# A two-layer hybrid decoder step: VectorE's order in two token mixers and the slots of four weight tiles

## What is computed

```python
z = rmsnorm(x) @ w_in                       # columns of four mixers and of their gates
oa = gla(z)        # gated linear attention: a decay for each key channel
ob = retnet(z)     # rotated q and k, a fixed decay for each head
oc = deltanet(z)   # convolution, then the gated delta rule with a triangular inverse
od = ssd(z)        # convolution, then a scalar decay for each head
x = x + (sum_n sigmoid(mg_n) * (o_n @ w_branch_n)) @ w_out
x = x + swiglu(x)  # layer 0 dense, layer 1 the best 2 of 8 experts
x = x + sigmoid(rmsnorm(x) @ ple_w_gate) * (p @ ple_w_proj)
```

## Time and profile before

| | us |
|---|---|
| median of 3 runs (lowest to highest) | 2600.65 (2597.46 to 2604.7) |
| the profiled execution, and its span in the trace | 2596.66, 2594.9 |
| TensorE busy | 2399.1 (92%), mean granted clock 0.944 |
| VectorE busy | 1639.1 (63%) |
| ScalarE busy | 1074.1 (41%) |
| GpSimd busy | 181.1 (7%) |

### The profile page before, as it was taken

One profiled execution on the slowest core, in us unless ns is written; L12 is line 12 of the kernel. 1 busy time (PEld: TensorE's weight loads), 2 busy tenths in 40 slices (PEclk: granted clock), 3 DMA queues, 4 the chain that ended last, 5 costly groups with the idle time before them and its releaser, 6 DMA issues.

```text
span 2594.9 us, 38245 instructions
## 1 busy us (share of the span) xinstructions
PE 2399.1 (92%) x14436; PEld 2069.6 (80%) x14436; DVE 1639.1 (63%) x2112; ACT 1074.1 (41%) x1450; POOL 181.1 (7%) x247
## 2 busy tenths in 40 slices
PE   8899898899999899899798997999999999999996
PEld 6788778876899888789687866787887878878786
DVE  4554853743665454457636633778787887878776
ACT  4332311321333334324122220566666666667662
POOL 0212111201000001202012010000000000000000
PEclk8999898998999989999898988899999999999998
DMA  5323311322444333234112320898898978889871
GB/s 197 105 87 134 131 66 41 111 82 98 152 163 163 127 130 106 95 134 142 54 50 83 110 73 32 325 327 289 300 329 297 335 284 303 319 296 332 291 278 64
DMA packets 122566, 456.43 MB, mean 176 GB/s; under 512 B 14056, under 2 KB 14474, under 8 KB 120018
## 3 DMA queue, kind: packets, MB, share of 16 engines
q1 hardware_dynamic: 118818, 432.66, 47.5%
q0 software_dynamic: 3632, 22.12, 2.4%
HBM read 443.72 MB, written 11.00 MB: 175 GB/s over the span
## 4 chain that ended last, share of the span: by engine, by line
PE 72%; DVE 17%; issue 6%; ACT 4%; POOL 1%; DVEq 0%; DMA 0%; SPq 0%; ACTq 0%; POOLq 0%
PE ps L726 7%; PE ps L728 7%; PE ps L727 7%; PE ps L773 6%; DVE weights_low L2255 4%; PE ps L1293 4%; PE ps L1295 4%; PE ps L1294 4%; PE ps L1315 3%; PE ps L1316 3%; PE ps L1317 3%; PE ps L1266 3%; PE ps L767 2%; DVE arena L1889 2%; PE ps L808 1%
## 5 line engine op out<-in xcount | busy, mean ns | idle before, releaser
L726 PE MATMUL ps<-u_high,tiles_high 128*128 128x288 f32 x1688 | 526.0, 312 | 17.5 <-DVE tiles_low L1718 17.5
L727 PE MATMUL ps<-u_low,tiles_high 128*128 128x288 f32 x1688 | 513.0, 304 | 0.0
L728 PE MATMUL ps<-u_high,tiles_low 128*128 128x288 f32 x1688 | 511.1, 303 | 0.0
L1718 DVE TENSOR_TENSOR tiles_low<-ring,tiles_high 128x1024 fp32r<-128x1024 f32 x238 | 298.1, 1255 | 201.6 <-ACT tiles_high L1374 200.2
L726 PEld LDWEIGHTS ps<-u_high,tiles_high 128*128 128x128 f32 x1688 | 332.1, 197 | 26.7 <-issue 24.6
L2255 DVE TENSOR_TENSOR weights_low<-expert_ring,weights_high 128x1024 fp32r<-128x1024 f32 x288 | 334.5, 1219 | 5.2 <-ACT weights_high L1627 2.0
L727 PEld LDWEIGHTS ps<-u_low,tiles_high 128*128 128x128 f32 x1688 | 332.6, 197 | 0.5
L728 PEld LDWEIGHTS ps<-u_high,tiles_low 128*128 128x128 f32 x1688 | 332.2, 197 | 0.0
L1374 ACT ACTIVATE tiles_high<-ring 128x1024 fp32r<-128x1024 f32 x238 | 250.6, 1054 | 170.9 <-DMA ring<-in_stream 81.0
L1293 PE MATMUL ps<-weights_high,u_high 128*128 128x512 f32 (+1 forms) x768 | 297.6, 388 | 22.9 <-DVE weights_low L2255 22.3
L2255 DVE TENSOR_TENSOR weights_low<-ring,weights_high 128x1024 fp32r<-128x1024 f32 x240 | 280.2, 1218 | 43.2 <-ACT weights_high L1627 42.1
(11 more groups left out here) (381 smaller groups left out, 3290.2 us busy)
## 6 DMA issues: line engine op xcount, KB each, us to landing
ring<-in_stream SPq DMA_DIRECT2D x530, 512.0 KB, 4.2
expert_ring<-in_stream SPq DMA_DIRECT2D x288, 512.0 KB, 5.6
arena<-in_state POOLq DMA_DIRECT2D x8, 1024.0 KB, 5.1
state_s<-arena POOLq DMA_DIRECT2D x8, 1024.0 KB, 4.3
const<-in_const SPq DMA_DIRECT2D x1, 2052.5 KB, 12.0
arena<-in_const POOLq DMA_DIRECT2D x2, 832.0 KB, 4.9
h<-in_x SPq DMA_DIRECT2D x1, 1152.0 KB, 5.0
y<-acc POOLq DMA_DIRECT2D x1, 1152.0 KB, 4.4
```

What stands on the lines that cost most here:

```text
L726: mm(out, hi[k], uh[:, k, :], start=k == 0, stop=False)
L727: mm(out, hi[k], ul[:, k, :], start=False, stop=False)
L728: last = mm(out, lo[k], uh[:, k, :], start=False, stop=k == KD - 1)
L1718: tt(t_low[:, q % HELD, :], ring[:, (t % RING) * TILE:(t % RING + 1) * TILE], t_high[:, q % HELD, :].bitcast(F32), ALU.subtract).then_inc( ...
```

## The change

VectorE in GLA takes the values and clears the banks right behind the first level's differences, ahead of the three lows of slot 0; `qg` and the clearing of `dd` come behind slot 0. VectorE in RET takes only the first of the three branch tiles of slot 0 ahead of the sines and the addition, and the other two behind them. Two slot lists are new. In GDN the tile of slot 29 goes to slot 27 and, dealt out in order, slot 30 gets a tile and slot 38 none. In SSD slots 2 and 5 become empty, slots 7 and 11 get a tile, and slots 13, 17 and 19 have the tile that was in 14, 16 and 18.

```diff
 SLOTS = [
     [3, 1, 2, 1, 1, 1, 1, 0, 1, 0, 1, 1, 1, 1, 1, 1, 1, 2],
     [3, 1, 1, 2, 1, 1, 2, 2, 1, 2],
-    [1, 1, 1, 1, 1, 1, 1, 1, 0, 1, 0, 0, 1, 1, 0, 1, 0, 1, 0, 1, 0, 1, 0, 1, 0, 1, 0, 0, 0, 1, 0,
-     0, 0, 0, 1, 0, 1, 1, 1, 0, 0],
-    [1, 1, 1, 1, 1, 1, 1, 0, 1, 1, 1, 0, 1, 0, 1, 1, 1, 0, 1, 0, 1, 2, 2],
+    [1, 1, 1, 1, 1, 1, 1, 1, 0, 1, 0, 0, 1, 1, 0, 1, 0, 1, 0, 1, 0, 1, 0, 1, 0, 1, 0, 1, 0, 0, 1,
+     0, 0, 0, 1, 0, 1, 1, 0, 0, 0],
+    [1, 1, 0, 1, 1, 0, 1, 1, 1, 1, 1, 1, 1, 1, 0, 1, 0, 1, 0, 1, 1, 2, 2],
 ]
...
-            def fill(L, n, s):
-                for x in FILL[L][n][s]:
+            def fill(L, n, s, lo=0, hi=None):
+                for x in FILL[L][n][s][lo:hi]:
                     lows(T_OF[x] - 1)
                     if x[0] == "br":
                         branch_tile(x)
...
                 for lv, w in enumerate(LEVELS):
-                    if lv == 1:
-                        take_vk(L, GLA)
-                        V.memset(ps_t[:, M:M + 4, 0:PAIR], 0.0).then_inc(cross_zero, 1)
-                        tt(qg[:, 0:2, :], zq[:, :, 256:288], egp[:, 0:2, :], ALU.mult).then_inc(qg_ready, 1)
-                        V.memset(dd, 0.0)
                     if lv >= 2:
                         dve.wait_ge(lev_ps, 6 * L + lv - 1)
...
                     last.then_inc(ldiff_ready, 1)
+                    if lv == 0:
+                        take_vk(L, GLA)
+                        V.memset(ps_t[:, M:M + 4, 0:PAIR], 0.0).then_inc(cross_zero, 1)
                     fill(L, GLA, lv)
+                    if lv == 0:
+                        tt(qg[:, 0:2, :], zq[:, :, 256:288], egp[:, 0:2, :], ALU.mult).then_inc(qg_ready, 1)
+                        V.memset(dd, 0.0)
...
-                fill(L, RET, 0)
+                fill(L, RET, 0, 0, 1)
                 dve.wait_ge(rot_ps, L + 1)
                 tt(z4, ps_t[:, M:M + 4, 0:TOK], C("sin").unsqueeze(1).to_broadcast([P, 4, TOK]), ALU.mult).then_inc(dve_step, 1)
                 dve.wait_ge(dve_step, steps.next())
                 tt(z4, z4, tmp4, ALU.add).then_inc(rope_ready, 1)
+                fill(L, RET, 0, 1)
                 dve.wait_ge(rope_ready, L + 1)
```

## The result

| | before | after |
|---|---|---|
| median of 4 runs each (lowest to highest) | 2600.67 (2597.46 to 2604.7) | 2615.56 (2610.8 to 2619.68) |
| ratio to before, 95% interval | | 1.0067 [1.0052, 1.0082] |
| profiled execution, span | 2596.66, 2594.9 | 2610.8, 2609.0 |
| TensorE busy | 2399.1 | 2417.0 |
| TensorE idle (span less busy) | 195.8 | 192.0 |

What follows compares the result with a forecast made beforehand. TensorE, busy for 92% of the span, was taken as the bound, so only idle time and clock could give anything back. Reorderings -8.7 and slots +8.1 a layer gave -1.2 us in two layers: 2599.5, range 2583 to 2609.

Steps and rivals of the forecast that it cites:

- GLA, -5.5 a layer: GLA's first level: the 4.0 us wait for bank clearing goes, and 1.5 of low clock behind it is regained.
- the low comes late: Rival in GLA: third tile's low late by 1.8, or second level by 1; 5.6 more, 2605.1, chance 0.06.
- the contention I bounded at 1.8: GLA: GpSimd's multiplying might hold VectorE off the values, starting the third tile 1.8 late; 0 was taken.
- I take 1.5 of it as regained: GLA: of 1.7 us lost at clock 0.72 behind the wait, 1.5 comes back without it (0 to 1.7).
- RET, -3.2: RET: TensorE's wait of 3.21 us ahead of the transposes, for the rotation's last step, goes whole in each layer.
- GDN, +0.6: GDN: wait of 1.11 and 2.54 moves one level; output norm's chain shifts +0.6 a layer (-2.0 to +2.6).
- SSD, +7.5: SSD slots, a layer: two tiles behind the convolution +6.4, clock +1.7, first outputs' wait +2.0; earlier start, low, wait -1.15, -1.15, -0.3.
- about 5.7 less what the low clock takes: SSD: TensorE's wait ahead of the transposes, 0.48 before, with two tiles moved behind the convolution.
- slots free: Rival: moved SSD tiles fill waits and cost nothing, only the reorderings count; -17.4, 2583.3, chance 0.24.
- my -0.6 a layer: Mixers, whole change: the two reorderings -8.7 and the slots +8.1 a layer, or -1.2 us in two layers.
- the likeliest case: Whole kernel: no change that a measurement can tell (about 0.3%, 7.8 us), 2599.5, chance 0.58.
- the clock goes the other way: Rival: low clock follows the moved waits in GLA, GDN and SSD; 4.9 a layer, 9.8 in all, 2609.3, chance 0.12.

Runs made afterwards that it cites:

- the run of GLA alone: Kernel before with only GLA's values and bank clearing early, RET's order and slot lists of before: 2596.53, ratio 0.9963 [0.9938, 0.9987].
- after again: The changed kernel, unchanged, run again beside three others on the same chip: 2614.23, ratio 1.0065 [1.0043, 1.0088] to the kernel before.
- after 4 later: The changed kernel with the first norm's reciprocal computed three times, 4 us more ahead of all work: 2617.23, ratio 1.0065 [1.004, 1.009].

## Why the prediction was wrong

**GLA, -5.5 a layer: the wait was right, the clock term failed.** The wait of 4.0 went (idle 11.2 to 6.9), the held-back low came in time, and "the low comes late" fell. Values were taken beside GpSimd's product at 1.23 us for the 1.22 of the earlier trace rows, so the contention I bounded at 1.8 is nothing; the rule of the Trainium skill that I weighed (SBUF — State Buffer, "Who interferes with whom") agrees with that. What failed is "I take 1.5 of it as regained": I read the low clock behind the wait as that wait's doing, which would go with it. Instead of -1.5, busy time rose by 4.1 and 7.1. In the two profiles, GLA lies 5.4 and 8.5 us a layer over the forecast, 13.9 of the 15.3 that the span lies over it. As a draw this is on the high side: over the 18 layers profiled with GLA's new order busy time was 104.9 on average (100.5 to 112.1), over the six with the old order 103.8 (102.3 to 109.6). That average puts the term at +1.1, not -1.5, and GLA at -3.1 a layer, which lies inside the interval of the run of GLA alone (-9.6, from -16 to -3, for two layers).

**RET, -3.2: right.** RET's stretch fell by 3.4 in both layers, its idle time from 14.8 to 11.6.

**GDN, +0.6: right in its wait, wrong in its clock.** The pair of 1.11 and 2.54 came one level later as 1.11 and 2.44. By the runs without and with the new GDN slots the stretch grows by 0.9 and 1.1 (150.1 to 151.0, 153.2 to 154.3), and SSD's convolution comes 1.2 and 1.1 earlier (40.1 and 40.0 to 38.9), where 1.15 was forecast. But these two runs are one pair: over all profiled layers the stretch took 153.5 on average with the new slots (16 layers) and 150.8 with the old (12, and other edits differ among them too). That is +2.7, all but 0.2 of it busy time, where I had -2.0 to +2.6: of the 2.6 of clock that I took off the tile's 3.2, some 0.5 shows. In after, layer 1 has 4.0 more busy time than layer 0 with the same idle time, again the clock.

**SSD, +7.5: right in size.** From the norm's sums to the first outputs the time grew by 6.6 and 4.7 in after, and by 6.6 in both layers of after again. Wait by wait: 7.14 ahead of the transposes, longer than "about 5.7 less what the low clock takes", 2.06 ahead of the first outputs for 2.0. The rival "slots free" is out.

**The sum.** Taken apart, my -0.6 a layer was +1.8 of idle time and -2.4 of clock (-1.5 in GLA, -2.6 in GDN, +1.7 in SSD). Measured: -1.5 and -2.3 of idle time, +5.7 and +10.4 of clock. The step that failed is this clock term: the prediction had the changed kernel granted a little more clock than before, and it was granted less (0.934 and 0.935 for 0.944 in the median). So the likeliest case lost to the rival "the clock goes the other way", for which I had 0.12 and 2609.3; its sign that the granted clock of the mixers is lower (0.91 before, 0.90 and 0.89 after) is there. Its price, 9.8 on top of the forecast, was too small for the 16.1 measured, as I let GLA only keep its loss. Its mechanism, low clock that follows the moved waits, isn't shown: in GLA the wait went, and the clock fell all the same.

**What stays open.** How the 16 us between forecast and result divide among the parts is not settled by the times: the reorderings came out 1.6 under their forecast gain, the slots 6.7 over their forecast price, and the two together 10 over their sum, none of which stands clear of its interval. That the miss is busy time, not idle time, is shown by the profiles, and that it goes with the granted clock by all executions. What makes one program draw low clock more often than another, and whether that of after draws more of it than its parts would give, stays open.

## What to carry to other kernels

Split every span into TensorE's busy and idle time before and after. Where TensorE sets the pace, as in GLA, idle time moves by what the waits say, to a few tenths, while busy time of the same instructions moves with the granted clock, and can take back all that a removed wait gave. Where another engine ends a stretch, as VectorE does with SSD's convolution, low clock fills the wait, and only the length tells. Don't book low clock behind a wait as part of that wait's price; give it both signs, as large as the wait itself, and take its size from several executions, not from one. Set executions at the same granted clock beside each other, where there are some. Test such parts together as well as apart: here the reorderings without the slots are the version to keep (2584.62, 0.6% under before).

## What the hardware showed that I had not expected

Low clock doesn't need a wait ahead of it. These are 46 us of layer 1, of the kernel after and of after 4 later, from 68 us behind GLA's transposes:

```profile
1080.30:1126.30 46.00, 45.65 (x345) 43.09 (x344) 22.44 (x13) 15.38 (x22) 6.64 (x6) 0.81 0.24 80
```

```profile
1079.90:1125.90 46.00, 45.50 (x377) 41.48 (x376) 23.63 (x17) 16.16 (x23) 7.48 (x7) 1.00 0.30 102
```

TensorE idles for 0.35 and 0.50 us in all, and is granted 0.81 in one and 1.00 in the other; it got 32 matmuls further at full clock. In the 28 us ahead of them both were granted 0.82 and idled for 4.6 and 3.1 us. The fall in the kernel after has nothing but work ahead of it. These are 10 us at full clock and the 20 us behind them, both without idle time:

```profile
1078.00:1088.00 10.00, 10.00 (x90) 9.55 (x89) 2.45 (x2) 3.43 (x6) 1.02 (x2) 1.00 0.66 233
1088.00:1108.00 20.00, 20.00 (x130) 19.56 (x129) 2.68 (x3) 6.10 (x10) 5.78 (x4) 0.74 0.16 54
```

Busy isn't the same as full: between 1084.8 and 1099.0 lie 64 matmuls of four columns each (L919). Whether these bring the clock down is not shown; after 4 later has them too, at full clock. The Trainium skill (TensorE: Matmul & The Clock Gate, "HAM oscillation — how this bites in real kernels") explains a fall of the clock by idle gaps between bursts of matmuls; here the measurement differs, as a stretch without idle time holds one. The Trainium skill (TensorE: Matmul & The Clock Gate, "What's actually happening") says that the monitor's window runs on its own and isn't reset when a kernel starts, which would fit the draws; no run here shows it.
